# Column loads in two parts, small loads behind the row roots, and other orders and passes in the mixer of a hybrid block

## The chip, the cores and the metric

The kernel runs on one core of a Trainium2 chip. The metric is the device time of one execution in microseconds (us); the number given for a kernel is the median of several runs. A profiled execution stands beside them, and all rows below are from it; their times count from the start of its span.

## The reference

One layer of a diffusion backbone works on 1024 latent tokens (a grid of 16 rows by 64) and 256 context tokens of width 1024, all in float32. Cut to what matters here:

```python
sx1, cx1, gx1, sx2, cx2, gx2 = split(silu(c) @ w_mod + b_mod, 6)   # the same for c_ctx
hx = rmsnorm(x, norm1) * (1 + cx1) + sx1                           # hc likewise
u, q, k, v, g, r = split(hx @ w_in)                                # one projection
pooled = concat([box_mean(box_mean(u[g], rows, w), columns, w) for g, w in enumerate((2, 4, 8, 16))]) - u
x = x + gx1 * (concat([pooled @ w_pool * pool_scale, gla(q, k, v, r) * silu(g)]) @ w_out)
x = x + gx2 * moe(rmsnorm(x, norm2) * (1 + cx2) + sx2)             # top 2 of 16 experts
out = rmsnorm(x, norm_f)
```

A box mean of window w sums the w neighbours of a place (fewer at the edges) and divides by their count, first down the 16 grid rows, then along the 64 columns.

## The kernel before

Each engine has its own program, written out by hand; semaphores order them. SP issues the large loads on one queue, GpSimd issues small ones on another.

**Modulation.** The columns of w_mod that give sx1 and cx1 come as four groups of 512 columns, 2 MB each (`load_mod(0..3)`). TensorE multiplies them by silu(c) (`modulation(j)`, L1400), ScalarE copies the result (`mod_out`), TensorE turns it (`turn_mod`). Rows 0 are squared and summed on ScalarE (`square(0)`, L659), their root is taken on GpSimd (L559, L562), VectorE scales the rows (`scale_rows`, L929), TensorE turns them (`turn_rows`, L1388), always in tiles of 128 tokens. SP's order is: groups 0 to 2, rows 0 and 1, group 3, part 0 of w_in, rows 2, part 1, rows 3 to 9. GpSimd builds constants first and then issues seven small loads (w_gk in two, b_gk, w_r, icnt, w_rt, bias_b) before it waits for the first row sum.

**Projections.** w_in is read in parts of 256 columns, and 54 projections n follow each other on TensorE (`proj(n)`, L1461 by rows and L1464 by columns): 0 to 19 values (two parts by ten token tiles), 20 to 27 the pooling's u, 28 to 33 keys, 34 to 37 queries, 38 to 53 gates. To keep float32 precision each operand is split: ScalarE copies it to a rounded high half (`part_high`, `hx_high`), VectorE subtracts (`part_low` L946, `hx_low` L942), and TensorE does three products, so that a projection has 24 matmuls. Projection 0 takes part 0 and tile 0, projection 1 part 1 and tile 0; each new tile is turned (`turn_rows`) after an even projection, tile 2 after projection 1. VectorE and ScalarE go through steps n beside TensorE, each with a fixed order inside a step.

**Late modulation.** The other eight groups of columns come in quarters. VectorE multiplies and adds them in the accumulator macc (`late_sum(q)`, L984 and L986), quarters 0 to 15 in steps 4 to 19, 16 to 31 two a step from step 20 on. TensorE sums the partitions (`late_turn(i)`, L1498) in steps 8, 12, 16, 20, 22, 24, 26 and 28, VectorE adds the bias (`late_row(i)`, L999) at the end of the step after, and GpSimd stores the row and loads the next bias. `late_turn(i)` waits for `late_row(i-1)` and for its sums.

**Pooling.** From step 30 on VectorE works through the pooling between its other work (`pool_steps`, three pieces a step, later one). For each window: copy into a padded tile, log2(w) additions down the rows (L1028), a product with the inverse counts of the rows (L1037), additions along the columns (L1044), a product with the inverse counts of the columns (L1048), a subtraction of u (L1052). Evacuations of keys (L1071) and queries (L1074) stand between; TensorE's next projections wait for their banks. Both products read counts that are the same inside and differ only near the edges.

The rest (the recurrence over chunks, scores, output projection, router, 31 blocks of experts at L1677, final norm) is not touched.

Of the kernel before, what the change touches and what calls it, by code (L numbers as in the profile page):

```python
# [30 lines left out]
P = 128  # L31
# [7 lines left out]
GRID_W = 64  # L39
# [35 lines left out]
def hybrid_block(nc, x, c, ctx_in, c_ctx, w_mod, b_mod, norm1, norm2, w_in, w_gk2, b_gk, w_pool,  # L75
                 pool_scale, gla_gain, w_out, w_router, router_bias, w1, w3, w2, norm_f, inv_counts, out):
    with ExitStack() as stack:
# [3 lines left out]
        def sem(name):  # L81
            return stack.enter_context(nc.semaphore(name))
# [79 lines left out]
        with nc.sbuf_tensor("lead_columns", [P, O_G + D], F32), \  # L162
# [71 lines left out]
            box_chain pooled mixp_done mixp_ready  # L234
            y_done gated x2_ready ss2_ready pow2_ready hx2_ready hx2_turned hx2T_ready logit_done rl_out
            r_chain route_ready rank_done slots_done tok_table table_ready
            tok_ready tok_seen dst_ready dst_seen high_seen split_seen load_seen gathered x_turned xh_ready xT_ready l1a_half l1a l1b l1c silu_done hid_a hid_b hta htb
            hTh_a hTh_b hT_a hT_b
            l2_half l2_done pads_stored x2_stored y_ready y_added y_free moe_done
            fss_ready fpow_ready fout_ready""".split()  # L240
        S = {n: sem(n) for n in names}

        row_loaded = [sem(f"row_loaded{t}") for t in range(NT)]
        mod_loaded = [sem(f"mod_loaded{j}") for j in range(4)]
        part_loaded, late_loaded, out_loaded = ([sem(f"{n}{i}") for i in range(2)] for n in ("part_loaded", "late_loaded", "out_loaded"))
        hx2_stored, stored = ([sem(f"{n}{i}") for i in range(2)] for n in ("hx2_stored", "stored"))

# [167 lines left out]
        def _(sp):  # L415
# [4 lines left out]
            def load_mod(j):  # L420
                sp.dma_start(early_mod[j], wmod_v[:, :, j * HALF:(j + 1) * HALF]).then_inc(mod_loaded[j], 16)

            def load_part(m):
                if m == 2:
                    sp.wait_ge(S["mod_turned"], 1)
                    sp.wait_ge(S["ss_ready"], NT)
                elif m >= 3:
                    sp.wait_ge(S["proj_done"], part_end[m - 2])
                col = parts[m][1]
                sp.dma_start(raw_for(m).rearrange("p (k n) -> p k n", k=KC), win_v[:, :, col:col + HC]).then_inc(part_loaded[m % 2], 16)  # L430
# [10 lines left out]
                load_mod(j)  # L441
            load_rows(0)
            load_rows(1)
            load_mod(3)
            load_part(0)
            load_rows(2)
            load_part(1)
            for t in range(3, NT):
                if t >= 8:
                    sp.wait_ge(S["turned"], t - 7)  # L450
# [14 lines left out]
            def load_expert(e, turn, first=False):  # L465

                for j, w in enumerate((w1, w3, w2)):
                    n = 3 * turn + j
                    if first and n < 2:
                        sp.wait_ge(S["y_done"], 2 * (NX - 1) + j + 1)  # L470
                    elif first and n == 2:
                        sp.wait_ge(S["pads_stored"], 16 * 2)
                        sp.wait_ge(S["x2_stored"], 16 * NX)
                        sp.wait_ge(S["hx2_ready"], NX)
                    elif not (first and n == 3):
                        sp.wait_ge(w_split[(j + 2) % 3], 2 * e - (2 if j == 0 else 0))
                        sp.sem_inc(S["split_seen"], 1)
                    if not (first and turn == 0):
                        sp.wait_ge(w_loaded[j], 16 * e)
                    k = KC if j < 2 else 4  # L480
                    sp.dma_start(raw[:, (n % PLACES) * UNIT:][:, 0:UNIT].rearrange("p (k n) -> p k n", k=k),
                                 w[0, bass.ds(e, 1)].rearrange("o (k p) n -> p (o k) n", p=P)).then_inc(w_loaded[j], 16)
# [21 lines left out]
        def _(pool):  # L504
# [32 lines left out]
            link(pool, cc, pool.iota(place_p[:, :], pattern=[[0, 1]], base=0, channel_multiplier=1,  # L537
                      allow_small_or_imprecise_dtypes=True))

            for d in range(2):  # L540
                pool.dma_start(w_gk[16 * d:16 * d + 16, d, :], w_gk2[0, d]).then_inc(S["gk_loaded"], 16)
            pool.dma_start(w_gk[32:33, :, :], b_gk).then_inc(S["gk_loaded"], 16)
            pool.dma_start(w_r[:, :, :], win_v[:, :, COL_R:COL_R + RANK2]).then_inc(S["rw_loaded"], 16)
            pool.dma_start(icnt[:, :, :].rearrange("p g n -> p (g n)"),
                           inv_counts.partition_broadcast(P)).then_inc(S["pool_w_loaded"], 16)
            pool.dma_start(w_rt[:, :, :], w_router.rearrange("(k p) e -> p k e", p=P)).then_inc(S["pool_w_loaded"], 16)
            pool.dma_start(bias_b[:, :], router_bias.rearrange("(o e) -> o e", o=1).partition_broadcast(P))\
                .then_inc(S["pool_w_loaded"], 16)

            def late_bias(i):  # L550
                if i >= 1:
# [5 lines left out]
            for t in range(NT):  # L557
                pool.wait_ge(S["ss_ready"], t + 1)
                pool.tensor_scalar(stat[:, NT + t:NT + t + 1], stat[:, t:t + 1], 1.0 / D, EPS, ALU.mult, ALU.add)\  # L559
                    .then_inc(S["box_chain"], 1)  # L560
                pool.wait_ge(S["box_chain"], t + 1)
                pool.tensor_tensor(stat[:, 2 * NT + t:2 * NT + t + 1], stat[:, NT + t:NT + t + 1], expo[:, 0:1], ALU.pow)\  # L562
                    .then_inc(S["pow_ready"], 1)
                pool.wait_ge(S["pow_ready"], t + 1)
                if t == 2:
                    late_bias(0)

            for i in range(1, 9):
                late_bias(i)
# [20 lines left out]
            def gather(b):  # L590
                pool.tensor_copy(block_tok[:, :], slot_tok[:, bass.ds(b, 1)]).then_inc(S["tok_ready"], 1)  # L591
                pool.wait_ge(S["tok_ready"], b + 1)
                pool.sem_inc(S["tok_seen"], 1)
                pool.indirect_dma_start(out=xg, out_offset=None, in_=hx_dram,
                                        in_offset=bass.IndirectOffsetOnAxis(ap=block_tok[:, :], axis=0))\
                    .then_inc(S["gathered"], 16)

            def add_rows(b, s):

                pool.tensor_copy(block_dst[:, :], slot_tok[:, bass.ds(b, 1)]).then_inc(S["dst_ready"], 1)  # L600
                pool.wait_ge(S["dst_ready"], b + 1)
                pool.sem_inc(S["dst_seen"], 1)
                pool.indirect_dma_start(out=x_dram, out_offset=bass.IndirectOffsetOnAxis(ap=block_dst[:, :], axis=0),
                                        in_=ysb[:, s, :], in_offset=None, compute_op=ALU.add).then_inc(S["y_added"], 16)

# [12 lines left out]
            with pool.Fori(0, NB // 2) as pair:  # L618
                i = pair * 2
                for s in range(2):  # L620
                    with pool.If(i + (s + 1) < nb):
# [2 lines left out]
                            pool.wait_ge(S["x_turned"], b + 2)  # L624
                            gather(b + 2)
                        pool.wait_ge(S["y_ready"], 2 * i + (2 * s + 6))
                        pool.sem_inc(S["dst_seen"], 1)
                        pool.wait_ge(S["y_added"], 16 * b)
                        pool.sem_inc(S["y_free"], 1)
                        add_rows(b, 1 - s)  # L630
# [11 lines left out]
        def _(act):  # L642
# [95 lines left out]
            hx_high(0)  # L738
            part_high(0, 1)
            hx_out(1)  # L740
            hx_high(1)
            square(2)
            part_high(1, 0)
            part_high(1, 1)
            square(3)
            for n in range(group_no[("g", 1, 0)]):
                if n in hx_at:
# [171 lines left out]
        def _(dve):  # L919
# [44 lines left out]
            hx_low(0)  # L964
            part_low(0, 1)
            hx_out(1)
            hx_low(1)
            part_low(1, 0)
            part_low(1, 1)
            scale_rows(2)  # L970
            sc = ("s_chain", [0])
# [42 lines left out]
            def pool_steps():  # L1014
                dve.wait_ge(S["pool_w_loaded"], 48)
                dve.wait_ge(S["proj_done"], group_no[("k", 1, 2)] + 1)
                for g, w in enumerate(WINDOWS):
# [8 lines left out]
                    while L <= w:  # L1026
# [7 lines left out]
                                   for b in (dst, src))  # L1034
                    link(dve, sc, dve.memset(wide[:, :, 8 - h:8], 0.0))
                    link(dve, sc, dve.memset(wide[:, :, 8 + GRID_W:8 + GRID_W + h], 0.0))
                    link(dve, sc, dve.tensor_tensor(  # L1037
                        wide[:, :, 8:8 + GRID_W], src[:, 8 - h:8 - h + GRID_H, :],
                        icnt[:, g, 0:GRID_H].unsqueeze(2).broadcast_to([P, GRID_H, GRID_W]), ALU.mult))
                    yield  # L1040
                    src, dst, L = wide, wide2, 2
                    while L <= w:
# [2 lines left out]
                                                        src[:, :, lo + L // 2:lo + L // 2 + n], ALU.add))  # L1045
                        src, dst, L = dst, src, 2 * L
                        yield
                    link(dve, sc, dve.tensor_tensor(  # L1048
                        dst[:, :, 0:GRID_W], src[:, :, 8 - h:8 - h + GRID_W],
                        icnt[:, g, GRID_H:].unsqueeze(1).broadcast_to([P, GRID_H, GRID_W]), ALU.mult))  # L1050
                    ug = uT[:, g, :].rearrange("p (r w) -> p r w", w=GRID_W)
                    dve.tensor_tensor(ug, dst[:, :, 0:GRID_W], ug, ALU.subtract).then_inc(S["pooled"], 1)  # L1052
                    dve.wait_ge(S["pooled"], g + 1)
                    yield

# [24 lines left out]
            for n in range(group_no[("g", 1, 0)]):  # L1080
# [7 lines left out]
                    scale_rows(scale_at[n])  # L1088
                if n in hx_at:
                    hx_low(hx_at[n])  # L1090
                if 0 <= n - LAG_C < NT:
                    softplus(n - LAG_C)
                for m, i in pieces_at.get(n, ()):
# [4 lines left out]
                if n >= pool_from:  # L1098
                    for _ in range(3 if n < group_no[("g", 0, 0)] else 1):
                        next(pooling, None)  # L1100
                if n - 1 in late_turn_at:
                    late_row(late_turn_at[n - 1])
            for _ in pooling:
                pass
            dve.wait_ge(S["mrow_stored"], 16 * 8)
# [202 lines left out]
            def low(j, base, e, k):  # L1308

                dve.wait_ge(w_high[j], 2 * e + (k + 1))  # L1310
                dve.sem_inc(S["high_seen"], 1)
                dve.tensor_tensor(half_of(j, w_lo[j][:, :], k), half_of(j, raw[:, bass.ds(base, UNIT)], k),  # L1312
                                  half_of(j, w_hi[j][:, :], k).bitcast(F32), ALU.subtract).then_inc(w_split[j], 1)

# [62 lines left out]
        def _(pe):  # L1377
# [14 lines left out]
            def modulation(j):  # L1392
# [4 lines left out]
                    pe.wait_ge(S["small_ready"], 1)  # L1397
                for k in range(KC):
                    g = k % 4
                    ins = pe.matmul(ps[RANK2 * g:RANK2 * (g + 1), 4 + j, :], silu_p[:, k, :], w[:, k, :], start=(k < 4), stop=(k >= 4))  # L1400
                ins.then_inc(S["mod_used"], 1)

# [351 lines left out]
```

## Time and profile before

| | |
|---|---|
| runs | 1001.66, 997.30, 998.83 us |
| median | 998.83 us |
| profiled execution | 1000.63 us, span 998.81 us |
| busy TensorE / VectorE / ScalarE / GpSimd | 904.7 / 612.5 / 391.3 / 190.7 us |
| mean granted TensorE clock | 0.941 of full |

The profiled execution has a time of its own, so a sum made from its rows is to be set against 1000.63. A row of a timeline gives the start, the duration, the engine, the line of the kernel, what is written and read, and in brackets how long the engine had been idle and who released it; "q" behind an engine's name is its queue of issued instructions.

### The profile page before, as it was taken

The page shows a single profiled execution, that of the slowest core. Times are in us where ns is not written, and L with a number is a line of the kernel's source. Part 1 is how long each engine was busy: PE and PEld are TensorE (multiplying, and loading weights), DVE is VectorE, ACT ScalarE, POOL GpSimd, SP SyncE. Part 2 cuts the span into 40 slices and gives each one's busy share as a digit, 9 for nine tenths or more (in the row PEclk, how much of TensorE's full clock was granted, in tenths as well). Part 3 has the DMA queues.
Part 4 walks back from the last instruction along what each step waited for, and adds up shares of the span by engine and source line. Part 5 has one row for each costly group of instructions (what it writes and reads, how often), then busy time and mean ns, then how long its engine had stood idle before and what let it go on. Part 6 is the DMA issues. An engine that isn't in the chain of part 4 may idle for free. (4 is left out here: it accounts for less than half of the span.)

```text
span 998.8 us, 15160 instructions
## 1 busy us (share of the span) xinstructions
PE 904.7 (91%) x5471; PEld 726.8 (73%) x5472; DVE 612.5 (61%) x804; ACT 391.3 (39%) x535; POOL 190.7 (19%) x210
## 2 busy tenths in 40 slices
PE   4799999989998999999828999999999999999960
PEld 1598876768888456565427988888889888888850
DVE  0466645569966344544368357669957546699934
ACT  1664455301021312111140336457735534577603
POOL 4111000000000011001001133324432233243323
PEclk9699999989999999999955999999999999999985
DMA  9923543611124421111474596969997688699828
GB/s 334 357 64 108 170 127 116 198 35 43 43 86 155 183 84 64 64 43 43 159 283 187 151 312 210 334 221 349 361 374 240 198 247 256 200 350 361 292 42 357
DMA packets 81136, 194.73 MB, mean 195 GB/s; under 512 B 3893, under 2 KB 12218, under 8 KB 81098
## 3 DMA queue, kind: packets, MB, share of 16 engines
q1 hardware_dynamic: 68736, 152.05, 43.3%
q0 software_dynamic: 7616, 25.34, 10.4%
q10 hardware_dynamic: 4746, 16.82, 4.4%
q8 instruction: 25, 0.41, 0.2%
q14 instruction: 13, 0.11, 0.0%
HBM read 168.50 MB, written 25.71 MB: 194 GB/s over the span
## 5 line engine op out<-in xcount | busy, mean ns | idle before, releaser
L1601 PE MATMUL ps<-arena 128*128 128x512 f32 x256 | 113.3, 595 | 0.0
L1677 PE MATMUL ps<-w3h,xTh 128*128 128x256 f32 x368 | 105.9, 288 | 0.0
L1677 PE MATMUL ps<-w3h,xTl 128*128 128x256 f32 x368 | 104.1, 283 | 0.0
L1677 PE MATMUL ps<-w3l,xTh 128*128 128x256 f32 x368 | 104.1, 283 | 0.0
L1601 PEld LDWEIGHTS ps<-arena 128*128 128x128 f32 x256 | 47.4, 190 | 54.4 <-issue 53.6
L1312 DVE TENSOR_TENSOR w1l<-raw,w1h 128x2048 fp32r<-128x2048 f32 x30 | 68.6, 2286 | 29.5 <-ACT w1h L842 29.5
L842 ACT ACTIVATE w1h<-raw 128x2048 fp32r (+1 forms) x32 | 61.1, 1913 | 58.6 <-PE ps L1677 52.8
L1677 PE MATMUL ps<-w2h,hTh 128*128 128x512 f32 x184 | 76.9, 418 | 1.2 <-DVE hTl L1325 0.9
L1677 PE MATMUL ps<-w1h,xTh 128*128 128x512 f32 x184 | 72.7, 395 | 3.3 <-DVE xTl L1305 3.3
L1677 PE MATMUL ps<-w1l,xTh 128*128 128x512 f32 x184 | 72.5, 394 | 0.0
L1677 PE MATMUL ps<-w1h,xTl 128*128 128x512 f32 x184 | 72.4, 393 | 0.0
L842 ACT ACTIVATE w2h<-raw 128x2048 fp32r (+1 forms) x32 | 61.1, 1918 | 28.8 <-PE ps L1677 21.5
L1677 PE MATMUL ps<-w2l,hTh 128*128 128x512 f32 x184 | 72.2, 392 | 0.0
L1677 PE MATMUL ps<-w2h,hTl 128*128 128x512 f32 x184 | 72.1, 392 | 0.0
L1312 DVE TENSOR_TENSOR w2l<-raw,w2h 128x2048 fp32r<-128x2048 f32 x32 | 71.7, 2283 | 0.0
L1677 PEld LDWEIGHTS ps<-w3l,xTh 128*128 128x128 f32 x368 | 70.5, 192 | 0.9
L1677 PEld LDWEIGHTS ps<-w3h,xTh 128*128 128x128 f32 x368 | 70.4, 191 | 0.9
L1312 DVE TENSOR_TENSOR w3l<-raw,w3h 128x2048 fp32r<-128x2048 f32 x31 | 70.9, 2286 | 0.0
L1677 PEld LDWEIGHTS ps<-w3h,xTl 128*128 128x128 f32 x368 | 70.5, 191 | 0.0
L842 ACT ACTIVATE w3h<-raw 128x2048 fp32r (+1 forms) x32 | 61.3, 1917 | 22.4 <-PE ps L1677 19.2
L1461 PE MATMUL ps<-high,hx_h 128*128 128x256 f32 x208 | 60.9, 293 | 2.7 <-DVE arena L1074 2.4
L591 POOL COPY block_tok<-slot_tok 128x1 int32 (+1 forms) x24 | 25.1, 1048 | 179.9 <-PE ps L1671 147.9
(270 smaller groups left out, 2024.8 us busy)
## 6 DMA issues: line engine op xcount, KB each, us to landing
raw<-in_w_dram SPq DMA_DIRECT2D x48, 2048.0 KB, 14.0
arena<-in_w_mod_dram SPq DMA_DIRECT2D x32, 512.0 KB, 3.8
arena<-in_w_mod_dram SPq DMA_DIRECT2D x4, 2048.0 KB, 15.8
arena<-in_w_in_dram SPq DMA_DIRECT2D x8, 1024.0 KB, 6.4
x_rows<-arena ACTq DMA_DIRECT2D x9, 512.0 KB, 2.6
hx_rows<-arena ACTq DMA_DIRECT2D x9, 512.0 KB, 2.7
arena<-in_x_dram SPq DMA_DIRECT2D x8, 512.0 KB, 12.7
arena<-in_w_out_dram SPq DMA_DIRECT2D x2, 2048.0 KB, 8.4
```

The lines of the kernel that those rows point to most:

```text
L591: pool.tensor_copy(block_tok[:, :], slot_tok[:, bass.ds(b, 1)]).then_inc(S["tok_ready"], 1)
L842: act.activation(half_of(j, w_hi[j][:, :], k), half_of(j, raw[:, bass.ds(base, UNIT)], k), ACT.Copy).then_inc(w_high[j], 1)
L1312: dve.tensor_tensor(half_of(j, w_lo[j][:, :], k), half_of(j, raw[:, bass.ds(base, UNIT)], k), half_of(j, w_hi[j][:, :], k).bitcast(F32), A ...
L1461: ins = pe.matmul(out_ap, hx[x_][:, t, k, :], w[w_][:, k, :], start=(k == 0 and i == 0), stop=(k == KC - 1 and i == 2))
L1601: ins = pe.matmul(ps[:, 5 + h, :], m, w[:, k, :], start=(k == 0), stop=(k == KC - 1))
L1677: ins = pe.matmul(out_ap, parts[l][:, lhs], w_parts[w][:, cols], start=start and n == 0, stop=stop and n == 2)
```

## The change

The fourth group of columns is loaded in two transfers of 1 MB, each with a semaphore, and TensorE waits for the second one only ahead of its half. Part 1 of w_in is loaded before rows 2. GpSimd's seven small loads are issued one at a time behind the row roots 3 to 9. ScalarE and VectorE take the two halves of part 1 earlier, around the high and low halves of tile 1 and ahead of row 2's square. `late_row` moves from the end of a step to a place ahead of the softplus, the splits and the late sums. In the pooling the products with whole count tiles become a product with the constant 1/w, and only the edge rows and columns, up to w/2 on the near side and w/2 - 1 on the far side, are multiplied by counts; the last product and the subtraction become one instruction. Four semaphores that only count are merged into one.

```diff
-        mod_loaded = [sem(f"mod_loaded{j}") for j in range(4)]
+        mod_loaded = [sem(f"mod_loaded{j}") for j in range(5)]
...
+            def load_last_mod(part):
+                ks = slice(4 * part, 4 * part + 4)
+                sp.dma_start(early_mod[3][:, ks, :], wmod_v[:, ks, 3 * HALF:4 * HALF]).then_inc(mod_loaded[3 + part], 16)
+
...
-            load_mod(3)
+            load_last_mod(0)
+            load_last_mod(1)
             load_part(0)
+            load_part(1)
             load_rows(2)
-            load_part(1)
...
                         sp.wait_ge(w_split[(j + 2) % 3], 2 * e - (2 if j == 0 else 0))
-                        sp.sem_inc(S["split_seen"], 1)
+                        sp.sem_inc(S["load_seen"], 1)
...
-            for d in range(2):
-                pool.dma_start(w_gk[16 * d:16 * d + 16, d, :], w_gk2[0, d]).then_inc(S["gk_loaded"], 16)
-            pool.dma_start(w_gk[32:33, :, :], b_gk).then_inc(S["gk_loaded"], 16)
-            pool.dma_start(w_r[:, :, :], win_v[:, :, COL_R:COL_R + RANK2]).then_inc(S["rw_loaded"], 16)
...
+            def small_load(t):
+                if t == 3:
+                    pool.dma_start(w_r[:, :, :], win_v[:, :, COL_R:COL_R + RANK2]).then_inc(S["rw_loaded"], 16)
+                elif t in (4, 5):
+                    pool.dma_start(w_gk[16 * (t - 4):16 * (t - 3), t - 4, :], w_gk2[0, t - 4]).then_inc(S["gk_loaded"], 16)
+                elif t == 6:
+                    pool.dma_start(w_gk[32:33, :, :], b_gk).then_inc(S["gk_loaded"], 16)
+                elif t == 7:
+                    pool.dma_start(icnt[:, :, :].rearrange("p g n -> p (g n)"),
+                                   inv_counts.partition_broadcast(P)).then_inc(S["pool_w_loaded"], 16)
+                elif t == 8:
+                    pool.dma_start(w_rt[:, :, :], w_router.rearrange("(k p) e -> p k e", p=P)).then_inc(S["pool_w_loaded"], 16)
+                elif t == 9:
+                    pool.dma_start(bias_b[:, :], router_bias.rearrange("(o e) -> o e", o=1).partition_broadcast(P))\
+                        .then_inc(S["pool_w_loaded"], 16)
...
                 pool.wait_ge(S["pow_ready"], t + 1)
                 if t == 2:
                     late_bias(0)
+                small_load(t)
...
             hx_out(1)
+            part_high(1, 0)
             hx_high(1)
+            part_high(1, 1)
             square(2)
-            part_high(1, 0)
-            part_high(1, 1)
             square(3)
...
             hx_out(1)
+            part_low(1, 0)
             hx_low(1)
-            part_low(1, 0)
             part_low(1, 1)
             scale_rows(2)
...
-                    link(dve, sc, dve.tensor_tensor(
-                        wide[:, :, 8:8 + GRID_W], src[:, 8 - h:8 - h + GRID_H, :],
-                        icnt[:, g, 0:GRID_H].unsqueeze(2).broadcast_to([P, GRID_H, GRID_W]), ALU.mult))
+                    rows_, edge = wide[:, :, 8:8 + GRID_W], src[:, 8 - h:8 - h + GRID_H, :]
+                    link(dve, sc, dve.tensor_scalar(rows_, edge, 1.0 / w, None, ALU.mult))
+                    for lo, hi in ((0, h), (GRID_H - h + 1, GRID_H)):
+                        if hi > lo:
+                            link(dve, sc, dve.tensor_tensor(
+                                rows_[:, lo:hi, :], edge[:, lo:hi, :],
+                                icnt[:, g, lo:hi].unsqueeze(2).broadcast_to([P, hi - lo, GRID_W]), ALU.mult))
...
-                    link(dve, sc, dve.tensor_tensor(
-                        dst[:, :, 0:GRID_W], src[:, :, 8 - h:8 - h + GRID_W],
-                        icnt[:, g, GRID_H:].unsqueeze(1).broadcast_to([P, GRID_H, GRID_W]), ALU.mult))
+                    sums = src[:, :, 8 - h:8 - h + GRID_W]
+                    for lo, hi in ((0, h), (GRID_W - h + 1, GRID_W)):
+                        if hi > lo:
+                            link(dve, sc, dve.scalar_tensor_tensor(
+                                out=sums[:, :, lo:hi], in0=sums[:, :, lo:hi], scalar=float(w),
+                                in1=icnt[:, g, GRID_H + lo:GRID_H + hi].unsqueeze(1).broadcast_to([P, GRID_H, hi - lo]),
+                                op0=ALU.mult, op1=ALU.mult))
                     ug = uT[:, g, :].rearrange("p (r w) -> p r w", w=GRID_W)
-                    dve.tensor_tensor(ug, dst[:, :, 0:GRID_W], ug, ALU.subtract).then_inc(S["pooled"], 1)
+                    dve.scalar_tensor_tensor(out=ug, in0=sums, scalar=1.0 / w, in1=ug, op0=ALU.mult, op1=ALU.subtract)\
+                        .then_inc(S["pooled"], 1)
...
                 if n in hx_at:
                     hx_low(hx_at[n])
+                if n - 1 in late_turn_at:
+                    late_row(late_turn_at[n - 1])
                 if 0 <= n - LAG_C < NT:
                     softplus(n - LAG_C)
...
-                if n - 1 in late_turn_at:
-                    late_row(late_turn_at[n - 1])
...
                 for k in range(KC):
                     g = k % 4
+                    if (j, k) == (3, 4):
+                        pe.wait_ge(mod_loaded[4], 16)
```

## Rows read from the trace of the kernel before

**Rows 1.** The page: TensorE's busy time, and its granted clock in 40 slices.
```profile
PE 904.7 (91%) x5471; PEld 726.8 (73%) x5472; DVE 612.5 (61%) x804; ACT 391.3 (39%) x535; POOL 190.7 (19%) x210
...
PEclk9699999989999999999955999999999999999985
```

**Rows 2.** Waits of TensorE, 0 to 300 us: total, times, longest.
```profile
PE ps L1400 <- DMA arena<-in_w_mod_dram: 5.5, 3, 3.1
PE ps L1498 <- DVE state L999: 4.2, 2, 3.9
PE ps L1461 <- DVE arena L1074: 2.4, 1, 2.4
```

**Rows 3.** Timeline of TensorE, 0 to 75 us: the four column groups.
```profile
9.24 3.64 PE L1400 MATMUL ps<-arena 128*32 128x512 f32 x16 [0.69 <-DMA arena<-in_w_mod_dram]
...
14.59 3.46 PE L1400 MATMUL ps<-arena 128*32 128x512 f32 x16 [1.70 <-DMA arena<-in_w_mod_dram]
...
22.09 3.64 PE L1400 MATMUL ps<-arena 128*32 128x512 f32 x16 [3.06 <-DMA arena<-in_w_mod_dram]
...
31.14 3.64 PE L1400 MATMUL ps<-arena 128*32 128x512 f32 x16
```

**Rows 4.** DMA queues, 10 to 26 us: GpSimd's queue.
```profile
q0 software_dynamic: 256, 0.40, 9.5%
```

**Rows 5.** Timelines of GpSimd and VectorE: w_r, root 4, scaling of row 4.
```profile
12.21 0.96 POOL L543 DMA_DIRECT2D rank_w<-in_w_in_dram  x1
...
50.36 0.71 POOL L559 TENSOR_SCALAR stat<-stat 128x1 f32<-128x1 f32 x1
...
58.84 0.75 DVE L929 TENSOR_SCALAR arena<-arena,stat 128x1024 f32<-128x1024 f32 x1
```

**Rows 6.** Timeline of all engines, 45 to 53 us: part 1's split.
```profile
45.70 2.00 ACT L686 ACTIVATE high_v<-arena 128x1024 fp32r<-128x1024 f32 x2
...
46.79 2.36 DVE L946 TENSOR_TENSOR low_odd<-arena,high_v 128x1024 fp32r<-128x1024 f32 x2 [0.91 <-ACT high_v L686]
...
48.07 0.39 PE L1461 MATMUL ps<-high_v,hx_h 128*128 128x256 f32 x1 [2.11 <-DVE low_odd L946]
...
51.36 0.41 PE L1461 MATMUL ps<-low_odd,hx_h 128*128 128x256 f32 x1
51.57 0.41 PE L1461 MATMUL ps<-high_v,hx_l 128*128 128x256 f32 x1
...
52.17 0.28 PE L1461 MATMUL ps<-high_v,hx_h 128*128 128x256 f32 x1
52.29 0.28 PE L1461 MATMUL ps<-low_odd,hx_h 128*128 128x256 f32 x1
```

**Rows 7.** Stretches: length, busy time of each engine, granted clock, DMA, GB/s.
```profile
38.30:44.80 6.50, 5.62 (x25) 5.25 (x26) 5.19 (x9) 5.15 (x10) 0.00 (x0) 0.50 1.03 412
...
48.50:51.80 3.30, 3.30 (x18) 3.30 (x17) 2.07 (x3) 1.67 (x5) 2.56 (x4) 0.50 0.02 7
...
202.10:208.80 6.70, 5.48 (x19) 3.81 (x20) 2.06 (x5) 0.00 (x0) 2.24 (x4) 0.50 0.06 8
209.00:260.00 51.00, 51.00 (x257) 43.50 (x256) 47.10 (x60) 6.07 (x7) 0.00 (x0) 1.00 0.15 46
```

**Rows 8.** Timelines of TensorE and VectorE, 186 to 206 us: the late modulation.
```profile
189.02 1.02 PE L1498 MATMUL ps<-wp,ones 128*1 128x512 f32 x2 [0.39 <-DVE state L999]
...
198.92 3.22 DVE L986 SCALAR_TENSOR_TENSOR wp<-arena,silu_c,wp 128x512 f32<-128x512 f32 x4
...
203.32 1.86 PE L1498 MATMUL ps<-wp,ones 128*1 128x512 f32 x2 [3.85 <-DVE state L999]
```

**Rows 9.** VectorE by line and form, 0 to 420 us: count, busy, mean ns.
```profile
L929 DVE TENSOR_SCALAR arena<-arena,stat 128x1024 f32<-128x1024 f32 x10 | 7.5, 747 | 20.7 <-POOL stat L562 20.7
...
L1141 DVE TENSOR_TENSOR arena<-arena 128x512 f32<-128x512 f32 x8 | 5.5, 692 | 0.3
...
L1037 DVE TENSOR_TENSOR arena<-arena,icnt 128x1024 f32<-128x1024 f32 x4 | 4.9, 1225 | 0.1
```

More of the change, by code:

```diff
@@ L236, in hybrid_block @@
             r_chain route_ready rank_done slots_done tok_table table_ready
-            tok_ready tok_seen dst_ready dst_seen high_seen split_seen load_seen gathered x_turned xh_ready xT_ready l1a_half l1a l1b l1c silu_done hid_a hid_b hta htb
+            tok_ready dst_ready load_seen gathered x_turned xh_ready xT_ready l1a_half l1a l1b l1c silu_done hid_a hid_b hta htb
             hTh_a hTh_b hT_a hT_b
@@ L538, in _ @@
                       allow_small_or_imprecise_dtypes=True))
-            for d in range(2):
-                pool.dma_start(w_gk[16 * d:16 * d + 16, d, :], w_gk2[0, d]).then_inc(S["gk_loaded"], 16)
-            pool.dma_start(w_gk[32:33, :, :], b_gk).then_inc(S["gk_loaded"], 16)
-            pool.dma_start(w_r[:, :, :], win_v[:, :, COL_R:COL_R + RANK2]).then_inc(S["rw_loaded"], 16)
[L544 to L548, printed above, removed]
+            def small_load(t):
[13 more added lines that the diff above has]
+                        .then_inc(S["pool_w_loaded"], 16)
             def late_bias(i):
@@ L592, in gather @@
                 pool.wait_ge(S["tok_ready"], b + 1)
-                pool.sem_inc(S["tok_seen"], 1)
+                pool.sem_inc(S["load_seen"], 1)
                 pool.indirect_dma_start(out=xg, out_offset=None, in_=hx_dram,
@@ L601, in add_rows @@
                 pool.wait_ge(S["dst_ready"], b + 1)
-                pool.sem_inc(S["dst_seen"], 1)
+                pool.sem_inc(S["load_seen"], 1)
                 pool.indirect_dma_start(out=x_dram, out_offset=bass.IndirectOffsetOnAxis(ap=block_dst[:, :], axis=0),
@@ L626, in _ @@
                         pool.wait_ge(S["y_ready"], 2 * i + (2 * s + 6))
-                        pool.sem_inc(S["dst_seen"], 1)
+                        pool.sem_inc(S["load_seen"], 1)
                         pool.wait_ge(S["y_added"], 16 * b)
@@ L1310, in low @@
                 dve.wait_ge(w_high[j], 2 * e + (k + 1))
-                dve.sem_inc(S["high_seen"], 1)
+                dve.sem_inc(S["load_seen"], 1)
                 dve.tensor_tensor(half_of(j, w_lo[j][:, :], k), half_of(j, raw[:, bass.ds(base, UNIT)], k),
```

## The prediction

> **What bounds the kernel now.** The page comes first: TensorE is busy for 91% of the span, and the clock row has dips at 25 to 50, 200 to 225, 500 to 550 us and at the end [rows 1]. So the kernel is bound by TensorE nearly everywhere, and a change is worth what it takes out of TensorE's idle time, or gives back of its clock. The list of what TensorE waited for in the first 300 us is short [rows 2]: 5.5 us for the modulation columns, 4.2 for VectorE's modulation rows (L999), 2.4 for a query evacuation (L1074); one more of that size, 2.1 for a low split (L946), is shown in its place [rows 6]. Everything that the change touches lies in these 300 us; behind them the work is released by what went before, so a gain there should arrive whole at the end.
>
> **The small loads.** The three first column groups are each 2 MB. TensorE starts on them at 9.24, 14.59 and 22.09 us [rows 3]: 5.35 us apart, then 7.50. From 10 to 26 us GpSimd's queue moves 0.40 MB in 256 packets, which take 9.5% of the engines' time [rows 4]. The change takes seven loads out of there. Upper bound: the second spacing becomes the first, 7.50 - 5.35 = 2.15 us. Lower bound: bytes alone, 0.40 MB at the rate of the undisturbed spacing (2.1 MB in 5.35 us, 392 GB/s), 1.0 us; the queue's packet time lies between, 0.095 x 16 = 1.5 us. I take 2.1, because the issues follow 10.4 us, so nearly all that they move falls into the longer interval (w_r's issue is at 12.21 [rows 5]). Nothing else in the chain behind is a transfer: the copy of the third group, the row squares, roots, scaling, the turn of rows 0 and the fourth group follow each other without a DMA wait, and the fourth group starts at 31.14 right behind the turn of rows 0, without a wait of its own [rows 3]. So **the split of the last columns** is worth 0 here: the work that hides it is that turn. Even 2.1 us earlier the columns, which move 2.1 us earlier too, are there. If its cover were gone it would give half of one 2 MB spacing, 2.7 us. Its cost is one more issue on SP, which is only filling queues then.
>
> The loads come back behind the row roots 3 to 9. Each stands on GpSimd's queue behind the root and ahead of the next root's two instructions. The w_r issue is the one with no room: it took 0.96 us, and root 4, at 50.36, began without an idle time before it [rows 5]. So root 4 comes 1 us later, done at about 52.7 in the old times, and its user, the scaling of row 4, ran at 58.84 [rows 5]. Cover 6 us before, some 3 us after the other shifts; cost 0. From root 5 on the rows come two projections apart, and a load's issue falls between them. w_r has its first reader behind projection 7, some seven projections of 3 us behind its new issue. The first logits and the pooling come later still. GpSimd's first store of a modulation row, which lies behind root 9, is delayed by one issue, under 1 us; the next row is written four projections (12 us) later. Cost 0.
>
> The Trainium skill (SBUF — State Buffer, the passage on VectorE blocking DMA) warns that a GpSimd-issued DMA has its descriptors written through a port that VectorE's fast modes lock, and gives 620 ns alone against some 3100 ns overlapped. By that figure root 4 would come about 3 us later, still just inside its cover, and the sum would not change; no row here shows an issue of that length.
>
> **First splits.** Projection 0 ends at 45.97 and TensorE waits until 48.07 for part 1's low split, which follows two ScalarE copies from 45.70 on; square(2) and hx_high(1) stand ahead of these [rows 6]. In the new order ScalarE does hx_out(1), part_high(1,0), hx_high(1), part_high(1,1), square(2). In the old times: 42.3, 43.4, 44.6, 45.7, 46.9. VectorE: hx_out(1) to 43.5, part_low(1,0) to 44.7, hx_low(1) to 45.9, part_low(1,1) to 47.1. Projection 1 needs the first half at 46.0 and the second half after 12 matmuls (2.5 us at the low clock). The 2.1 us wait is gone. What is late next is row 2: its square ends 1.2 us later than before, the root at 47.9, the scaling at 48.8, wanted at the end of projection 1 (49 to 51): just in time. Row 2's load lies behind 1 MB more, half a spacing, 2.7 us, less the 2.1; TensorE, ScalarE and VectorE show no wait for a row's transfer here [rows 2, 6].
>
> The granted clock was low (0.50, that is 1.2 GHz) from 38.3 to 44.8, though TensorE worked 5.62 of these 6.5 us; projection 0 ended at the full one (2.4 GHz), and after the pause from 45.97 to 48.07 it was low again from 48.5 to 51.8 [rows 7]. A matmul of 256 columns follows the last after 0.21 us at the low clock (51.36, 51.57) and after 0.12 at the full one (52.17, 52.29) [rows 6]. Without the pause that second low stretch has no reason to come. Starting 2.1 us earlier, projection 0 lies wholly in the first low stretch: 24 x 0.211 = 5.1, from 39.0 to 44.1; then 4 low matmuls and 20 full ones to 47.5. Before, projection 1 ended at 52.5. That is 5.0 earlier, 2.1 of it the start, so **2.9** for the split. Bounds: both projections low throughout, 10.1 against 11.4, a gain of 1.3; the rise one stretch earlier, limited by the split at 45.0, 3.8.
>
> **Row sums.** VectorE's late_row moves from the end of a step to ahead of its splits and sums. It costs nothing itself: eight short instructions in either order. TensorE's wait at 189.02 (0.4) was for late_row(5), which stood behind its step's split and sums although its own input, late_turn(5), was two projections old [rows 8]; it goes. The long one, 3.85 up to 203.32, is cut only in part: late_turn(7) also needs the sums that end at 202.14 [rows 8], and these follow the step's low split, that follows ScalarE's copy, and that the end of a projection on TensorE itself. It began 1.2 us after them; 0.2 is the hand-over, and the row and its gap, 1.0 us, are taken off. Some 2.9 us of the wait remain. Each row now has a step or more before the next one, so that stores and bias loads are in time. Together **1.4**. Behind the long wait the clock was low from 202.1 to 208.8 [rows 7], 3.3 us lost. A shorter wait may leave all, half or none of it: the pause of 2.1 us at 46 was followed by a low clock, but after the one of 2.4 us for L1074 [rows 2] the slices of the page stay at 9 [rows 1]. I take **1.0**, bounds 0 and 3.3.
>
> **Pooling.** TensorE waits 2.4 us for the evacuation L1074 [rows 2], which stands on VectorE behind the pooling; VectorE is busy for 47.1 of the 51 us from 209 to 260 [rows 7]. Before: three full passes of 1.225 us for each of four windows (L1037; L1048 and L1052 have its size and form) [rows 9]. After: one tensor_scalar (0.747 by L929, the same size [rows 9]), one scalar_tensor_tensor (1.22, no gain) and 14 edge passes. From 0.692 at 512 and 1.225 at 1024 elements [rows 9] a pass costs 0.16 us plus 1.04 ns an element, and 0.04 for each link. Windows 2, 4, 8, which are done ahead of that evacuation: rows 704 elements in 5 passes, 1.53; columns 176 in 5 passes, 0.98; links 0.4. Saved are 3 x 0.478 = 1.43 and 3 x 1.225 = 3.68. Net 5.11 - 2.91 = 2.2 us. Window 16 alone loses 0.3 (960 row elements), behind that evacuation, where the list has no further wait of TensorE for the pooling [rows 2]. So the wait shrinks by **2.1** and is almost gone. If the tensor_scalar ran at the full 1.225, the net is 0.8; a cheaper edge pass can't bring over 2.4. The Trainium skill (VectorE: DVE Perf Modes, the section on the TRN2 errata) says that each pass pays a fixed latency and many small tiles pay it again and again, which speaks against 14 edges; its formula, (N+151)/0.96 ns, an estimate that gives 0.16 fixed, leads to the same 2.2.
>
> **Sum.** 2.1 + 2.9 + 1.4 + 1.0 + 2.1 = 9.5 us. The profiled execution took 1000.63 us (span 998.81, 1.8 around it), so its like is 991.1; it was 1.8 above the median of the three runs, which gives 998.83 - 9.5 = **989.3 us**.
>
> **Rivals.** A, only the stalls go (chance 0.19): the transfers give their byte bound 1.0, the clock stays as it was at both places (1.3 of the split, 0), the row sums 1.4, pooling 0.8. 4.5 us: 994.3, range 993.8 to 997. For it speaks that three terms hang on the clock or on one spacing; against it that the 2.1 us pause is certain to go. B, the waits are merely moved (0.05): TensorE meets row 2's scaling or DMA-bound sums later by as much as it is earlier; 998.8. Against it: behind the modulation columns TensorE has no wait for a transfer in these 300 us, and none for the rows' scaling [rows 2]. C, the other side (0.04): the edge passes. If each strided edge cost like a full pass, 1.225, the ten ahead of the evacuation would add 12.25 + 0.4 and save 5.11, VectorE is 7.5 us later, and this eats the other 7.4. At 1.8 us an edge it is 13.3 later, and with 1.7 us of low clock behind the stall the time is 998.8 - 7.4 + 13.3 + 1.7 = 1006. It decides from 1.25 us an edge. Against it: 512 elements, more than most edges have, cost 0.692 [rows 9].
>
> **Chances.** The forecast has 0.72, its own range is 985.5 (upper bounds 0.9 more on the split, 2.3 on the clock, 0.3 on pooling) to 993.8. Measurements of this kernel tell a change from none at about 0.5%, 5 us, so 993.8 and 1003.8 are the borders. Faster: 0.72 and 0.05 of A's lucky end, 0.77; same: 0.19; slower: 0.04. The range 985 to 995.5 leaves out a third of A, B and C and what lies beyond both bounds.
>
> **What would show it.** The third column group starts near 19.9 us; the fourth waits for no transfer. No pause of TensorE between projections 0 and 1, projection 1 over by 47.5, full clock from about 45 on. w_r's issue under 1 us. late_turn(6) without wait, late_turn(7) with one of 2.9. L1074's wait below 0.5; the tensor_scalar at 0.75, edges between 0.18 and 0.7. Wrong it would be if the spacing stays 7.5, if row 2's turn waits, if the clock falls elsewhere, or if the gain at 300 us is not there at the end.

## The result and the profile after

| | before | changed |
|---|---|---|
| median of 6 runs each | 999.27 us (997.21 to 1001.66) | 988.86 us (986.37 to 989.26) |
| profiled execution, span | 1000.63, 998.81 us | 989.26, 987.5 us |

The ratio is 0.9889, 95% interval 0.987 to 0.9907, which is 11.1 us less (9.3 to 13.0); the two medians as they stand differ by 10.4, the two profiled executions by 11.4. The forecast was 989.3 with a gain of 9.5.

What TensorE still waits for in the first 290 us of the changed kernel (total, times, longest):

```profile
PE ps L1423 <- DMA arena<-in_w_mod_dram: 4.2, 2, 2.5
PE ps L1521 <- DVEq L1003: 4.1, 2, 2.9
...
PE ps L1409 <- DVE arena L941: 1.7, 1, 1.7
...
PE ps L1484 <- DVE arena L1095: 0.4, 1, 0.4
...
PE ps L1484 <- DVE low_odd L958: 0.3, 1, 0.3
```

The kernel before had, beside the waits of [rows 2], one for sums of the late modulation:

```profile
PE ps L1498 <- DVEq L991: 1.3, 1, 1.3
```

So the late modulation cost 4.2 for rows and 1.3 for sums, and now costs 4.1, all for sums (L1003 only counts behind them): 1.2 of the old wait and 2.9 at late_turn(7). The query evacuation took 2.4 and takes 0.4, part 1's split 2.1 [rows 6] and 0.3. The modulation columns took 5.5 and take 4.2, but this sum can't be read as the gain: the third group starts 2.2 us earlier although the wait ahead of it shrank only from 3.06 to 2.52, because the second group ran in 1.92 us instead of the 3.46 of [rows 3] and TensorE stood idle for the rest. Next, the places on TensorE's timeline (start, duration, in brackets idle time and releaser):

```profile
14.51 1.92 PE L1423 MATMUL ps<-arena 128*32 128x512 f32 x16 [1.68 <-DMA arena<-in_w_mod_dram]
...
19.93 3.49 PE L1423 MATMUL ps<-arena 128*32 128x512 f32 x16 [2.52 <-DMA arena<-in_w_mod_dram]
...
26.99 1.97 PE L1409 MATMUL ps<-ident,arena 128*128 128x128 f32 x8 [1.69 <-DVE arena L941]
...
28.89 2.43 PE L1423 MATMUL ps<-arena 128*32 128x512 f32 x16
...
43.63 0.39 PE L1484 MATMUL ps<-high_v,hx_h 128*128 128x256 f32 x1 [0.29 <-DVE low_odd L958]
...
45.17 1.03 PE L1409 MATMUL ps<-ident,arena 128*128 128x128 f32 x8
...
181.12 1.02 PE L1521 MATMUL ps<-wp,ones 128*1 128x512 f32 x2
...
194.46 1.86 PE L1521 MATMUL ps<-wp,ones 128*1 128x512 f32 x2 [2.89 <-DVEq L1003]
...
253.89 0.39 PE L1484 MATMUL ps<-high,hx_h 128*128 128x256 f32 x1 [0.40 <-DVE arena L1095]
```

The third group follows the second by 5.42 us (before 7.50 [rows 3]); the fourth still starts behind the turn without a wait. The bracket of 43.63 is the pause of [rows 6], those of 181.12 (none) and 194.46 are the waits of [rows 8]. Subtracting these times from those of before gives the ledger, in us by which the same work starts earlier: third group 2.2 (22.09 to 19.93), start of projection 0 3.4 (41.12 to 37.67), end of projection 1 7.4 (52.53, the turn behind its last matmul of [rows 6], to 45.17), late_turn(6) 7.9, late_turn(7) 8.9 (203.32 to 194.46), 8.6 behind the low clock that follows it, 10.5 at the query evacuation (264.43 to 253.89), 11.4 at 318 us, behind a boundary where the clock was low for 3.4 us instead of 6.9, and 11.3 at the end of the span. The granted clock in stretches (length, busy time of each engine, clock, DMA, GB/s):

```profile
28.89:29.90 1.01, 1.01 (x9) 0.35 (x12) 0.00 (x0) 0.00 (x0) 0.00 (x0) 0.50 1.09 346
30.10:31.32 1.22, 1.21 (x12) 0.12 (x4) 0.00 (x0) 0.00 (x0) 0.00 (x0) 1.00 1.16 360
37.70:40.20 2.50, 2.50 (x12) 2.50 (x13) 2.50 (x6) 2.17 (x6) 0.00 (x0) 0.50 1.02 408
40.40:46.00 5.60, 5.31 (x46) 5.11 (x44) 3.87 (x4) 5.34 (x9) 2.10 (x5) 1.00 1.02 391
...
194.00:200.60 6.60, 6.14 (x22) 4.43 (x23) 1.69 (x4) 0.00 (x0) 1.28 (x2) 0.50 0.18 51
```

At projections 0 and 1 the clock is low only up to 40.2 and full from 40.4 on: the second low stretch of [rows 7] is gone. In the fourth group it rose half way, for which the forecast had no term. Behind the shortened wait for late_turn(7) it is low for as long as before (193.8 to 200.7, before 202.1 to 208.9).

Of the seven small loads w_r is the one with a root right behind it (GpSimd's timeline):

```profile
45.71 0.56 POOL L573 TENSOR_TENSOR stat<-stat,expo 128x1 f32<-128x1 f32 x1
46.59 1.01 POOL L547 DMA_DIRECT2D rank_w<-in_w_in_dram  x1 [0.32 <-POOL stat L573]
47.68 0.18 POOL L570 TENSOR_SCALAR stat<-stat 128x1 f32<-128x1 f32 x1
47.94 0.56 POOL L573 TENSOR_TENSOR stat<-stat,expo 128x1 f32<-128x1 f32 x1
```

VectorE's scaling of row 3, which began ahead of the issue:

```profile
46.30 0.75 DVE L941 TENSOR_SCALAR arena<-arena,stat 128x1024 f32<-128x1024 f32 x1 [1.26 <-POOL stat L573]
```

And the pooling's passes, VectorE by line and form (count, busy, mean ns), against [rows 9]:

```profile
L1050 DVE TENSOR_SCALAR arena<-arena 128x1024 f32<-128x1024 f32 x4 | 2.8, 694 | 0.1
...
L1053 DVE TENSOR_TENSOR arena<-arena,icnt 128x512 f32<-128x512 f32 x1 | 0.7, 693 | 0.0
...
L1053 DVE TENSOR_TENSOR arena<-arena,icnt 128x64 f32<-128x64 f32 x2 | 0.5, 226 | 0.1
...
L1067 DVE SCALAR_TENSOR_TENSOR arena<-arena,icnt 128x16 f32<-128x16 f32 x2 | 0.4, 186 | 0.1
```

### The profile page after: what moved, and what is told of

Its sections match the earlier page's. It is cut to its first block and busy times, and to the rows that moved or that the text cites. A ratio compares the mean times of both kernels' runs of the same rounds, so it can differ in the third digit from the quotient of the medians.

```text
span 987.5 us, 15165 instructions
## 1 busy us (share of the span) xinstructions
PE 897.0 (91%) x5471; PEld 721.7 (73%) x5472; DVE 610.2 (62%) x814; ACT 391.4 (40%) x535; POOL 191.3 (19%) x210
## 5 line engine op out<-in xcount | busy, mean ns | idle before, releaser
L1624 PEld LDWEIGHTS ps<-arena 128*128 128x128 f32 x256 | 47.4, 190 | 54.4 <-issue 53.6
## 6 DMA issues: line engine op xcount, KB each, us to landing
raw<-in_w_dram SPq DMA_DIRECT2D x48, 2048.0 KB, 11.1
```

Source lines behind the costliest of these rows:

```text
L1624: ins = pe.matmul(ps[:, 5 + h, :], m, w[:, k, :], start=(k == 0), stop=(k == KC - 1))
```

## The experiments

The kernels were timed in three sessions, each beside the kernel before on the same chip. The level of the kernel before differs between the sessions (999.84, 1001.14 and 1001.23 us), so ratios compare with it, and kernels of one session are compared with each other by their medians. A statement on waits or on the clock is about the one profiled execution of a kernel.

**One part alone, on the kernel before.** Small loads: the seven issues moved as in the change, nothing else.

```diff
+                small_load(t)
```

> Only the small loads behind the row roots. My theory: the third column group starts at about 19.9 us instead of 22.09, nothing else on the way is a transfer, so 2.2 us less, and up to 1.2 more where the clock is granted earlier: 996 to 997.5 against 999.3. Rival A (only the bytes count): 1.0 us less, third group at 21.0. Rival B (the wait moves to the fourth group or to rows): the first projection starts at 41.1 as before, no change. The pause of 2.1 us ahead of projection 1 stays in both.

Measured: ratio 0.9971 (0.996 to 0.9981), 2.9 us less (1.9 to 4.0). The third group started at 19.83, so the spacing is 5.42 here too, and the fourth without a wait. The pause ahead of projection 1 stayed (2.3 us). Projection 0 started at 37.76 instead of 41.12, 3.4 us earlier, because the third and fourth groups ran partly at the full clock (2.80 and 3.34 us instead of 3.64 each). The 1.0 of rival A and the 0 of rival B lie outside the interval, and neither start time is theirs. Why 0.40 MB holds a transfer of 2 MB up by more than their bytes and their packet time stays open; no kernel here takes the loads away one by one.

First splits, with part 1 loaded ahead of rows 2:

```diff
+            part_high(1, 0)
             hx_high(1)
+            part_high(1, 1)
             square(2)
-            part_high(1, 0)
-            part_high(1, 1)
```

> Only the order of the first splits, with part 1 loaded ahead of rows 2; the small loads stay where they were. My theory: the pause of 2.1 us ahead of projection 1 shrinks below 0.5, the clock does not fall behind it, so 2.9 to 3.9 us less: 995.4 to 996.5. Rival A: the pause goes but the clock is as low as before, 1.3 us less. Rival B: TensorE waits for the scaling of row 2 instead, no change.

Measured: ratio 0.9961 (0.9947 to 0.9974), 3.9 us less (2.6 to 5.3). The pause is gone altogether, and so is the second low stretch of the clock (stretches):

```profile
38.00:44.60 6.60, 5.60 (x25) 5.24 (x26) 6.42 (x11) 6.20 (x11) 0.00 (x0) 0.51 1.03 410
44.80:50.00 5.20, 5.20 (x45) 5.15 (x45) 3.43 (x4) 4.63 (x10) 2.78 (x6) 1.00 0.64 239
```

The first stretch is as low as in [rows 7], but the clock does not fall again after it. Rival A (1.3 us) lies outside the interval, and the turn of row tile 2 began without a wait at 48.43, so that rival B is out too.

Row sums: only late_row moved.

> Only late_row earlier in its step. My theory: late_turn(6) without a wait, the long wait of late_turn(7) 2.9 instead of 3.85, the clock behind it as low as before: 1.4 us less, 997.9. Rival: the shorter wait spares half of the low clock, 3 us less. Rival on the other side: the row now waits for its bias load ahead of the sums, so that late_turn is later, 1 us more.

Measured: ratio 0.9993 (0.998 to 1.0006), 0.7 us less, between 2.0 less and 0.6 more: too small to be told from nothing by its time. Its trace shows what it does: late_turn(6) has no wait, that of late_turn(7) is 2.9, and the clock was low for half as long as in [rows 7], from 201.5 to 204.9, and full after that:

```profile
198.30:201.10 2.80, 0.00 (x0) 0.00 (x0) 2.40 (x4) 0.00 (x0) 0.00 (x0) 1.00 0.75 262
201.80:205.00 3.20, 3.20 (x13) 2.37 (x12) 0.87 (x2) 0.00 (x0) 1.28 (x2) 0.52 0.01 1
205.20:208.00 2.80, 2.80 (x20) 2.54 (x20) 1.10 (x5) 0.00 (x0) 0.00 (x0) 1.00 0.30 99
```

Pooling: only the constant products and the edge passes.

> Only the pooling with constant products and edge passes. My theory: VectorE 2.2 us earlier at the evacuation for which TensorE waits 2.4, so 1.7 to 2.1 less: 997.4. Rival: the wait is not the whole story, the evacuations before it get later or the saved time is idle, no change. Rival C: strided edge passes cost like full ones, 7 us more.

Measured: ratio 0.9972 (0.9961 to 0.9983), 2.8 us less (1.7 to 3.9); TensorE's wait for the query evacuation is 0.4 instead of 2.4. Rival C, 7 us more, is out. The four parts add to 10.3 us, beside 11.1 (9.3 to 13.0) for the whole: within the noise, nothing is lost between them.

**One part undone, on the changed kernel.** The fourth group in one transfer:

```diff
-            load_last_mod(0)
-            load_last_mod(1)
+            load_mod(3)
...
-                    if (j, k) == (3, 4):
-                        pe.wait_ge(mod_loaded[4], 16)
```

> The changed kernel with the fourth column group in one transfer again. My theory: its cover, the turn of rows 0, is still there, the columns land before 28.9 us, so no change against the changed kernel, 988.9 within 1.5. Rival: the first half is what TensorE starts on, the fourth group waits for its transfer by up to 2.7 us, 991.5.

Measured: 987.88 us (ratio 0.987, 0.9855 to 0.9886), no slower than the changed kernel (0.9889). The group started at 28.98 behind the turn of rows 0 at 27.09, without a wait.

The splits in their old order:

```diff
-            part_high(1, 0)
             hx_high(1)
-            part_high(1, 1)
             square(2)
+            part_high(1, 0)
+            part_high(1, 1)
```

> The changed kernel with the old order of the first splits on ScalarE and VectorE; the loads stay in the new order. My theory: the pause of about 2 us ahead of projection 1 comes back and with it perhaps a low stretch of the clock: 2 to 3.9 us above the changed kernel, 991 to 993. Rival: the earlier start alone had made up for it, under 1 us more.

Measured: 990.60 us (ratio 0.9891, 0.9873 to 0.9908), 2.7 above the kernel with one transfer, the nearest kernel of the same session. The two intervals overlap, and the ratio is also that of the changed kernel itself, so the time alone does not show the loss. The trace, which is of the slowest of the four runs (993.28), does: the pause is back, on TensorE's timeline:

```profile
44.96 0.58 PE L1484 MATMUL ps<-high_v,hx_h 128*128 128x256 f32 x1 [2.55 <-DVE low_odd L958]
```

and the clock is low again behind it, so that projections 0 and 1 take 12.2 us (38.01 to 50.25) instead of 7.5 (stretches):

```profile
44.60:50.90 6.30, 5.94 (x28) 5.94 (x29) 2.86 (x4) 2.46 (x5) 3.70 (x7) 0.50 0.30 101
```

**The rest of the long wait.** The forecast left 2.9 us of wait ahead of late_turn(7), because its sums hang on TensorE's own last projection. So the last turn is put one projection later, and two:

```diff
-        late_turn_at = {QUARTERS[4 * i + 3] + 1: i for i in range(8)}
+        late_turn_at = {(29 if i == 7 else QUARTERS[4 * i + 3] + 1): i for i in range(8)}
```

> The changed kernel with the last late_turn after projection 29 instead of 28. The sums that it needs are then 2.9 us old, as long as the wait was. If the wait is what lowers the clock from 193.9 to 200.7 us, both go: 2.9 plus 3.4, 6.3 us below the changed kernel, 982.6. Rival: the clock falls there for another reason, only 2.9 less, 986. Other rival: VectorE, not TensorE, then sets the pace in the pooling, and the wait for the query evacuation L1095 grows by what was gained: under 1 us less.

> The same one step later, after projection 30, with a cover of 5.6 us more. My theory: as last_turn_29, 982.6, or up to 0.5 lower where a rest of the wait is left there. Rival: late_row and the load of the pooling weights behind it come so late that VectorE has a wait in the pooling, 1 to 2 us above last_turn_29.

Measured: 983.92 us (0.9828, 0.9815 to 0.9842) after projection 29, and 985.03 (0.9851, 0.9832 to 0.987) after 30; the two can't be told apart. A second time, beside other kernels:

> The kernel of last_turn_29 once more, as the base of this call: 6 us below the changed kernel, 0.983 of the kernel before.

Measured: 983.46 us, 0.9829 (0.9814 to 0.9844). The first measurement is 4.0 us below the kernel with one transfer of its session; by the ratios, which lie in different sessions, both are 6 below the changed kernel. The stretch on which it turns, over what was the low stretch:

```profile
191.00:194.40 3.40, 3.40 (x30) 3.30 (x28) 3.09 (x5) 0.00 (x0) 0.00 (x0) 1.00 0.80 275
194.60:201.00 6.40, 6.40 (x26) 4.57 (x25) 5.17 (x13) 0.00 (x0) 1.59 (x2) 1.00 0.13 44
```

TensorE has no pause, and the clock stays full. In all six profiled executions with the later turn (these three and the three below) it is full from 182 to 214 us; in all eight that have the wait it falls in the wait or within 1.4 us behind it. So the wait is what lowers the clock there, and it has two prices: its own 2.9 us, and half of the time at the low clock, 3.4 us where that lasts 6.8 and 1.7 where it lasts 3.4. The expectation of 6.3 took the longer one from the changed kernel's profile; the kernel with one transfer has the shorter, 4.6 in all, near the 4.0 measured. The time alone would not rule out a gain of only 2.9, as the first rival had it; the clock does. The rival in which VectorE then holds TensorE up is out: the wait for the query evacuation is still 0.4.

**Three more on this base.** The whole product with the counts down the rows, as before the change; the columns keep their edges:

> last_turn_29 with the old whole product with the counts down the rows; the columns keep the edges. By the rows of the changed kernel the row part costs more than it saves: 0.69 and 0.23 to 1.35 us of edges against 1.225, over the four windows 5.7 and 0.3 of links against 4.9. My theory: VectorE has 1.1 us less to do, TensorE's rest of a wait in the query evacuation (0.4) goes, at most 0.4 us less, so no change that can be measured. Rival: the constant product with the fast mode is what made the pooling cheaper, and the wait grows by 0.5 us and more.

Measured: 983.01 us (0.9823, 0.9807 to 0.9839), no difference from its base. TensorE's 0.4 us of wait for the query evacuation is gone, so VectorE is not later but a little earlier there. The row half of the pooling edit brings nothing, as the prediction's own terms had it (1.43 saved, 1.53 for the edges); the column half, where a whole pass was merged away and the edges are 16 to 128 elements, is the gain.

The second late turn one projection later (`13 if i == 1`):

> last_turn_29 with the second late_turn after projection 13 instead of 12, where TensorE waits 1.2 us for its sums. My theory: the next quarter's sums start only when it is done, so VectorE waits for TensorE and reaches the low halves of the next tile later; TensorE then waits there for about as long, no change or up to 2 us more. Rival: as for the last turn, the 1.2 us go.

Measured: 984.77 us (0.9837, 0.9821 to 0.9853), no gain, 1.3 above its base and not clear of noise. The wait of 1.2 us for the sums is gone, a new one of 0.6 stands at the turn of a row tile whose scaling is late (first row), because VectorE waited 3.0 us for the moved turn (second row), 1.35 in the base:

```profile
PE ps L1409 <- DVE arena L941: 0.6, 1, 0.6
```

```profile
92.10 0.49 DVE L996 TENSOR_SCALAR wp<-arena,silu_c 128x512 f32<-128x512 f32 x1 [3.00 <-PE ps L1521]
```

All seven small loads in a row behind root 3:

```diff
-                small_load(t)
+                if t == 3:
+                    for i in range(3, 10):
+                        small_load(i)
```

> last_turn_29 with all seven small loads issued in a row behind root 3 instead of one behind each root. They take 5.0 us of GpSimd, so root 4 comes 4 us later, at 52.4, and the scaling of row 4 at 52.4 instead of 51.9; TensorE wants it at 55.5. My theory: no change, what counts is that they are behind the columns, not that they are spread. Rival: the scaling and the low half of tile 3 behind it are late, TensorE waits 0.5 to 2 us.

Measured: 984.91 us (0.9834, 0.9818 to 0.9851), 1.4 above its base, not clear of noise. Root 4 followed root 3 by 5.8 us (46.45 to 52.24) instead of 2.2, with 4.6 us of issues between them, and the scaling of row 4, over by 53.6, still came in time for its turn at 56.60; TensorE has no wait for a scaled row from 36 to 285 us:

```profile
46.45 0.56 POOL L573 TENSOR_TENSOR stat<-stat,expo 128x1 f32<-128x1 f32 x1
47.33 1.01 POOL L547 DMA_DIRECT2D rank_w<-in_w_in_dram  x1 [0.32 <-POOL stat L573]
...
52.24 0.56 POOL L573 TENSOR_TENSOR stat<-stat,expo 128x1 f32<-128x1 f32 x1
```

```profile
52.83 0.75 DVE L943 TENSOR_SCALAR arena<-arena,stat 128x1024 f32<-128x1024 f32 x1
```

## Why the prediction was right, step by step

**What bounds the kernel: right.** What was taken out of TensorE's idle time in the first 290 us arrived at the end: 8.9 us at late_turn(7), 10.5 with the query evacuation, 11.3 at the end of the span. The 0.8 between the last two came from the clock at a boundary at 313 us, not from the change's own terms.

**Small loads, 2.1: right.** 2.16 us at the third group (the spacing fell from 7.50 to 5.42), and not the 1.0 of the bytes. In the changed execution another 1.2 us came in the fourth group, since the clock rose in the middle of it (2.43 us instead of the 3.64 of [rows 3]). The sum had no term for it, and the kernel with one transfer, whose fourth group took 3.64 us, has the same time within the noise; so it belongs to the single execution. The cover of root 4, put at some 3 us, was there: w_r's issue took 1.01 us, against the forecast's "under 1", and even 4.6 us of issues ahead of root 4 did not reach TensorE. The 3100 ns of the Trainium skill (SBUF — State Buffer) for an issue beside VectorE did not show: the scaling of row 3, 0.75 us from 46.30 on, reached 0.46 us into the issue that began at 46.59, and the issue was only 0.05 us longer than in [rows 5].

**Split of the last columns, 0: right,** by the kernel with one transfer.

**First splits, 2.9: right in kind, low in size for this execution.** From the start of projection 0 to the end of projection 1 it was 11.4 us and is 7.5, so 3.9, just above the upper bound (3.8); alone 3.9 (2.6 to 5.3). The forecast held the first low stretch where it was in time, up to 44.8, so that the earlier projection 0 would lie wholly inside it. The clock rose at 40.2 instead, in the middle of projection 0: the stretch moved earlier with the work. The 0.3 us of wait that remain come with that: TensorE was ready for the second half of part 1 before VectorE. Projections 0 and 1 take 7.5 us with the splits alone and 7.6 with one transfer as well. But 3.9 is not what the order is worth in each execution: in those of row sums alone and pooling alone, which keep the old order and its pause but have no second low stretch, they took 9.9 us, so that the new order would bring 2.4. Row 2 was just in time: its scaling ended at 45.05, its turn began at 45.17.

**Row sums, 1.4: right in the trace,** 0.4 and 1.0 (3.85 to 2.89); by time alone not resolved (0.7).

**The clock behind it, 1.0: open in a single execution.** In the four profiled executions with a wait of 3.9 us (before, loads alone, splits alone, pooling alone) the clock was low for 6.7 to 6.8 us, in those with 2.9 us for 6.9 once (the changed kernel) and for 3.3 or 3.4 three times (row sums alone, one transfer, splits undone). So the changed kernel's own profile shows a gain of 0, the others 1.7. The 1.0 was chosen between 0 and 3.3 and not worked out from a row, so that it came near is in part luck. That the wait is the cause of this low stretch is shown by the six executions without it.

**Pooling, 2.1: right.** 2.36 to 0.40 is 2.0. The fit of two rows, 0.16 us and 1.04 ns an element, met the edges: 0.226 at 64 elements (0.227), 0.693 at 512 (0.692), 0.186 at 16 (0.177). The rule of the Trainium skill (VectorE: DVE Perf Modes, TRN2 errata) that many small tiles pay a fixed cost each time shows in the row half: beside a constant product of 0.69 us a window has edges of 0.23 (one of 64) to 1.32 us (512 and 448), in place of one pass of 1.225. The kernel with the whole product is no different in time.

**The sum.** 9.5 was forecast, 11.1 measured (9.3 to 13.0). In the profiled execution the difference is 11.3: 1.0 more by the splits, 1.2 by the clock in the fourth group, 0.8 by the clock at 313 us, less the 1.0 that was put behind late_turn(7) and 0.3 more that was lost there (8.9 to 8.6). So terms without a place in the sum and a term that did not come partly cancel, which is luck. That the medians agree to 0.4 us owes something to the kernel before as well, whose six runs have a median 0.4 above that of the three shown. The upper bounds add to 3.5, so the lower end of the forecast's own range should have read 985.8 and not 985.5; nothing hangs on it.

**The better version.** With the last turn after projection 29 the kernel takes 0.983 of the time before, 4.0 us under the kernel with one transfer beside it, and 6 under the changed one by the ratios.

## What to carry to other kernels

Where one engine is busy for 91%, list its waits and price each at its own length and at the clock that follows it; here a wait of 2.9 us and the low clock behind it fell together when one turn was moved behind one more projection. Before a wait is shortened, follow the second thing that it waits for: an earlier late_row took only 1.0 of 3.9 us, because the sums came 1.0 us before it. Small loads on another queue cost the large one more than their bytes here (2.2 against 1.0 us), and it was enough to put them behind it; spreading them brought nothing that could be measured.

## What was not expected of the hardware

The same source of work met the full clock at different points: projection 0 began to run at the full clock 2.5 us after its start in the changed kernel and 3.5 us after it with the splits alone. A wait of 2.9 us was followed by a low clock of 3.3 to 3.4 or of 6.9 us, one of 3.9 us always by 6.7 to 6.8, and one of 2.4 us at the query evacuation by none. The pause ahead of projection 1 was followed by a low stretch in three executions (before, small loads alone, splits undone) and by none in two (row sums alone, pooling alone), where the clock stayed full from 44.5 and 42.8 us on; the pauses with none behind them were not the shorter ones (2.7 and 2.6 us beside 2.1, 2.3 and 2.5). In none of the nine profiled executions without that pause (0.3 us or less) did a second low stretch come up to 56 us. So at this place the low stretch needs the pause, but the pause does not always bring it; what decides is open. The six runs of the changed kernel differ by 3 us (986.4 to 989.3), and such places may be where, but only one of the six has a profile, so this is not shown.
